# Merging two 256-column products into one of 512 columns in 18 dense halves of a decoder trunk

## The reference

```
x_n = rms_norm(x);  h = x_n @ w_in                     # 1024 x 9216
y_a = (a_gb * conv3(a_gc * a_val)) @ w_out_a
u   = conv31(glu_val * sigmoid(glu_gate)) + conv_b_b
y_b = silu(layer_norm(u)) @ w_out_b + b_out_b
y_x = cross_attention(q, rms_norm(mem), w_kv) @ w_out_x
merged = g0 * y_a + g1 * y_b + g2 * y_x                # g = sigmoid(h_gate + b_gate)
x = x + merged @ w_o
x = x + hierarchical_moe(rms_norm(x));  out = rms_norm(x)
```

## Time and profile before

| | us |
|---|---|
| median of three runs | 865.9 |
| profiled execution | 865.89 |
| its span, first to last instruction | 864.1 |
| PE busy | 850.9 (98%) |
| DVE busy | 786.9 (91%) |
| ACT busy | 648.4 (75%) |
| POOL busy | 25.4 (3%) |

### The profile page before, as it was taken

How to read it: one execution, slowest core, us unless ns; L and a number is a source line. 1 busy time by engine, 2 the same in 40 slices (tenths; PEclk the granted TensorE clock), 3 DMA queues, 4 the chain that set the end, 5 groups by cost and what they waited for, 6 DMA issues and landing times.

```text
span 864.1 us, 14576 instructions
## 1 busy us (share of the span) xinstructions
PE 850.9 (98%) x5734; PEld 753.0 (87%) x5734; DVE 786.9 (91%) x779; ACT 648.4 (75%) x631; POOL 25.4 (3%) x33
## 2 busy tenths in 40 slices
PE   9999999999999999999999999999999999999996
PEld 6999999999889999877788888888888888888874
DVE  6458999999987786789999999999999999999996
ACT  6563424344454366588999999999999999999996
POOL 0110000000000000017000000000000000000000
PEclk9999999999999999999999999999999999999999
DMA  9962555445452359647999999999999999999971
GB/s 355 428 222 98 194 194 195 174 159 179 173 195 98 133 177 420 234 182 267 393 421 431 424 430 429 426 429 430 428 427 431 429 426 432 429 425 430 429 308 49
DMA packets 20743, 270.68 MB, mean 313 GB/s; under 512 B 2272, under 2 KB 2528, under 8 KB 4448
## 3 DMA queue, kind: packets, MB, share of 16 engines
q1 hardware_dynamic: 20144, 268.31, 76.1%
q10 hardware_dynamic: 560, 1.84, 0.5%
HBM read 269.08 MB, written 1.05 MB: 313 GB/s over the span
## 4 chain that ended last, share of the span: by engine, by line
PE 84%; DVE 12%; issue 2%; DMA 1%; ACT 0%; SPq 0%; DVEq 0%; ACTq 0%
PE ps L1614 24%; PE ps L1628 12%; PE ps L1428 9%; PE ps L1430 9%; PE ps L1429 9%; PE ps L1599 4%; PE ps L1638 3%; DVE lo L1132 3%; DVE lo L857 2%; DVE conv L956 2%; PE ps L1444 2%; PE ps L1445 2%; PE ps L1443 2%; PE ps L1712 2%; PE ps L1719 1%
## 5 line engine op out<-in xcount | busy, mean ns | idle before, releaser
L1132 DVE TENSOR_TENSOR lo<-raw,hi 128x2048 fp32r<-128x2048 f32 x142 | 320.1, 2295 | 0.3 <-ACT hi L670 0.3
L670 ACT ACTIVATE hi<-raw 128x2048 fp32r<-128x2048 f32 x141 | 264.8, 1914 | 15.7 <-PE ps L1614 15.7
L459 ACT ACTIVATE hi<-raw 128x2048 fp32r<-128x2048 f32 x62 | 118.6, 1914 | 58.4 <-PE ps L1430 37.6
L857 DVE TENSOR_TENSOR lo<-raw,hi 128x2048 fp32r<-128x2048 f32 x61 | 139.3, 2287 | 20.2 <-ACT hi L459 18.9
L1428 PE MATMUL ps<-inA,hi 128*128 128x256 f32 x544 | 155.0, 285 | 1.4 <-DVE lo L857 1.4
L1614 PE MATMUL ps<-hi,xeT 128*128 128x512 f32 x384 | 154.4, 402 | 0.2
L1429 PE MATMUL ps<-inA,hi 128*128 128x256 f32 x544 | 153.9, 283 | 0.0
L1430 PE MATMUL ps<-inA,lo 128*128 128x256 f32 x544 | 153.9, 283 | 0.0
L1614 PE MATMUL ps<-lo,xeT 128*128 128x512 f32 x384 | 150.2, 391 | 0.0
L1132 DVE TENSOR_TENSOR lo_last<-raw,hi_last 128x2048 fp32r<-128x2048 f32 x48 | 110.3, 2298 | 0.0
L1428 PEld LDWEIGHTS ps<-inA,hi 128*128 128x128 f32 x544 | 104.4, 192 | 2.5 <-DVE lo L857 2.4
(11 more groups left out here) (259 smaller groups left out, 1291.8 us busy)
## 6 DMA issues: line engine op xcount, KB each, us to landing
raw<-in_w_experts SPq DMA_DIRECT2D x96, 2048.0 KB, 12.2
raw<-in_w_dense SPq DMA_DIRECT2D x28, 2048.0 KB, 7.8
raw<-in_w_dense SPq DMA_DIRECT2D x3, 1024.0 KB, 12.1
x_sb<-in_x SPq DMA_DIRECT2D x2, 512.0 KB, 3.6
raw<-in_w_dense SPq DMA_DIRECT2D x2, 512.0 KB, 7.7
mem_sb<-in_mem SPq DMA_DIRECT2D x1, 1024.0 KB, 15.7
x_again<-in_x ACTq DMA_DIRECT2D x1, 1024.0 KB, 17.4
out<-x SPq DMA_DIRECT2D x3, 256.0 KB, 2.1
```

The costliest lines, as they stand in the source:

```text
L459: return nc.scalar.activation(conv_half(hi, N), raw_half(slot, h), ACT.Copy)
L670: nc.scalar.activation(expert_half(hi, N0), raw_flat(slot, k % 2), ACT.Copy).then_inc(hi_made, 1)
L857: nc.vector.tensor_tensor(conv_half(lo, N), raw_half(slot, h), conv_half(hi, N).bitcast(f32), ALU.subtract).then_inc(lo_made, 1)
L1132: nc.vector.tensor_tensor(expert_half(lo, N0), raw_flat(expert_slot(m), k % 2), expert_half(hi, N0).bitcast(f32), ALU.subtract).then_inc(l ...
```

## The change

- `inA` and `inB` become [k, part, position], so that a k tile's high and low part are 512 neighbouring columns.
- In the halves named in `WIDE` (2 to 7 and 44 to 55) `wide_columns` takes the place of `columns`: the weight's high part is multiplied with both activation parts at once, 512 columns that fill a whole PSUM bank, and the weight's low part with the activation's high part, 256 columns, into the bank's first half. A half then has 32 products instead of 48, and its result lies in two banks, in two column halves that have to be added.
- The six banks are used as three pairs by the wide halves (`bank_pair`).
- The sum: ScalarE copies the second column half out (for glu_value and out_b with the bias) and counts `low_part`; VectorE adds the first column half and frees the banks. For glu_gate and gate1 ScalarE then applies the sigmoid to the sum, behind `dense_hi(n + 3)`. VectorE's product with the gate reads SBUF.
- In a wide step VectorE makes `lo` of half n + 2 before it takes the half's result, not behind it, and `ln_variance` goes ahead of both.

```diff
+WIDE = [n for n in range(2, DENSE) if UNITS[n // 2][0] in ("glu_value", "glu_gate", "out_x", "gate1", "out_b")]
-        inA = at("inA", A0, [2, KT, T], r32)
+        inA = at("inA", A0, [KT, 2, T], r32)
...
+            def wide_columns(N, acts):
+                w_hi, w_lo = conv_half(hi, N), conv_half(lo, N)
+                for c in range(2):
+                    bank = ps[:, 2 * bank_pair(N) + c, :]
+                    for k in range(KT):
+                        mm(bank, w_hi[:, k, c * P:(c + 1) * P], acts[:, k, :, :].rearrange("p x t -> p (x t)"),
+                           start=(k == 0), stop=False, skip_group_check=True)
+                        last = mm(bank[:, 0:T], w_lo[:, k, c * P:(c + 1) * P], acts[:, k, 0, :],
+                                  start=False, stop=(k == KT - 1), skip_group_check=True)
+                last.then_inc(half_used, 1)
... (ScalarE)
+                elif name == "gate1":
+                    act.wait_ge(merged_x, 4)
+                    nc.scalar.activation(gate[:, two, :], wide_half(n, 1), ACT.Copy).then_inc(low_part, 1)
...
                 elif name == "out_b":
+                    act.wait_ge(half_used, n + 1)
...
+                    for k in range(2):
+                        last = nc.scalar.activation(part[:, k, :], wide_half(n, 1)[:, k, :], ACT.Identity,
+                                                    bias=vec("b_out", 2 * q4 + k))
+                    last.then_inc(low_part, 1)
                     act.wait_ge(merged_all, q4 + 1)
...
                 if n + 3 <= DENSE + 1 and n != F["gate1"] + 1:
                     dense_hi(n + 3)
+                if name in ("glu_gate", "gate1"):
...
+                    act.wait_ge(gate_summed, gate_sums(n) + 1)
+                    for k in range(2):
+                        last = nc.scalar.activation(gate[:, 2 * q4 + k, :], gate[:, 2 * q4 + k, :], ACT.Sigmoid,
+                                                    bias=vec(vector_, 2 * q4 + k, k0))
... (VectorE)
+                if n in WIDE:
+                    dense_lo(n + 2)
+                    b = 2 * bank_pair(n)
...
+                    dve.wait_ge(low_part, WIDE.index(n) + 1)
+                    nc.vector.tensor_tensor(dst, wide_half(n, 0), dst, ALU.add).then_inc(bank_free[b], 1)
...
-                if not (name == "w_o" and n % 2 == 1):
+                if n not in WIDE and not (name == "w_o" and n % 2 == 1):
                     dense_lo(n + 2)
```

More of the change, by code:

```diff
@@ L255, in sums, with bank_pair, banks_of, bank_uses @@
             return ps[:, 2 * t:2 * t + 2, :].rearrange("p a b -> p (a b)")
+        def bank_pair(n):
+            return (n - 1) % BANK_PAIRS
+        def banks_of(n):
+            return (2 * bank_pair(n), 2 * bank_pair(n) + 1) if n in WIDE else (n % RING,)
+        def bank_uses(n, b):
+            return sum(b in banks_of(m) for m in range(n))
+        def wide_half(n, part_):
+            b = 2 * bank_pair(n)
+            return ps[:, b:b + 2, part_ * T:(part_ + 1) * T]
         def raw_slot(u):
@@ L440, in _, with gate_sums @@
             ins.then_inc(rounds_made, 1)
+        def gate_sums(n):
+            return sum(UNITS[m // 2][0] in ("glu_gate", "gate1") for m in WIDE if m < n)
         def stage_of(n):
@@ L660, in _ @@
                     dense_hi(n + 3)
+                if name in ("glu_gate", "gate1"):
+                    vector_, k0, made = ("b_glu", 1, glu_gate) if name == "glu_gate" else ("b_gate", 1, gate_made)
+                    act.wait_ge(gate_summed, gate_sums(n) + 1)
+                    for k in range(2):
+                        last = nc.scalar.activation(gate[:, 2 * q4 + k, :], gate[:, 2 * q4 + k, :], ACT.Sigmoid,
+                                                    bias=vec(vector_, 2 * q4 + k, k0))
+                    last.then_inc(made, 1)
                 for work in extra.get(n, ()):
@@ L1046, in _ @@
                 two = slice(2 * q4, 2 * q4 + 2)
-                if name in ("a_c", "a_b", "out_a", "out_x", "out_b"):
+                if name in ("a_c", "a_b", "out_a"):
                     dve.wait_ge(half_used, n + 1)
+                if n in urgent:
+                    urgent[n]()
+                if n in WIDE:
+                    dense_lo(n + 2)
+                    b = 2 * bank_pair(n)
+                    dst = part[:, :, :] if name in ("out_x", "out_b") else (u_sb if name == "glu_value" else gate)[:, two, :]
+                    dve.wait_ge(low_part, WIDE.index(n) + 1)
+                    nc.vector.tensor_tensor(dst, wide_half(n, 0), dst, ALU.add).then_inc(bank_free[b], 1)
+                    dve.wait_ge(bank_free[b], bank_uses(n, b) + 1)
+                    dve.sem_inc(bank_free[b + 1], 1)
+                    if name == "glu_value":
+                        dve.sem_inc(glu_value, 1)
+                    elif name in ("glu_gate", "gate1"):
+                        dve.sem_inc(gate_summed, 1)
                 if name == "a_c":
@@ L1080, in _ @@
                     dve.wait_ge(gate_made, 8 + q4 + 1)
-                    for k in range(2):
-                        c = 2 * q4 + k
-                        link(nc.vector.scalar_tensor_tensor(part[:, k, :], bank2[:, k, :], vec("b_out", c),
-                                                            gate[:, c, :], ALU.add, ALU.mult))
-                    dve.sem_inc(bank_free[b], 1)
+                    link(nc.vector.tensor_tensor(part[:, :, :], part[:, :, :], gate[:, two, :], ALU.mult))
                     nc.vector.tensor_tensor(merged[:, two, :], merged[:, two, :], part[:, :, :], ALU.add).then_inc(merged_all, 1)
```

128 lines of the change are left out of this document (73 added, 55 removed).

## The result

The changed kernel takes **876.94 us**, median of 5 runs (874.97 to 878.61), against 865.9 before: a ratio of 1.0129, 95% interval 1.0119 to 1.0140. It is slower, as forecast, but by 11.0 us instead of 6.5, and the time lies outside the range of 868.5 to 875.5. The runs differ by 3.6 us among themselves, where those of the kernel before differ by 1.5, and their order is that of the mean granted clock: 878.61 and 878.40 us at 0.988, 876.94 at 0.992, 875.21 and 874.97 at 0.995.

What follows compares the result with a forecast made beforehand. TensorE was taken to bound the dense part. Against 865.89 us: -3.8 products, -0.4 old wait, +5.7 first wait, +3.5 second wait, +1.4 clock, +0.1 restarts, in all +6.5, so 872.4 us; range 868.5 to 875.5.

Steps and rivals of the forecast that it cites:

- The clock: Gap before half 52: granted clock falls late in it, a quarter of half 52's 5.5 us at half rate, +1.4 us.
- the clock stays up: Rival: no fall of the clock in the gap before half 52, all else as forecast, 871.0 us; chance 0.30.
- The products: 18 halves (2 to 7, 44 to 55): each 5.55 us instead of 5.76, 0.21 less, in all -3.8 us.
- The old wait: Before half 49: TensorE's wait for VectorE's remainder goes, as that is now made ahead of the sum, -0.4 us.
- the restart: Before half 49: 0.1 us for TensorE to start again after its wait there.
- The first wait: Before half 52: TensorE waits for `lo`, late behind gate1's sigmoids and half 49's sum, +5.7 us.
- The second wait: Before half 57: out_b's merges turn every 6.96 us against TensorE's 5.55, so TensorE waits, +3.5 us.
- The front halves: Halves 2 to 7: they lose nothing of the 1.25 us that their wider products save.
- One to one: End of the dense part: its delay moves the experts' start by as much; their stage keeps its length within a microsecond.

Runs made afterwards that it cites:

- the products grouped: Changed kernel, but each column block runs its eight 512-column products first, then its eight 256-column ones, instead of alternating: 875.77 us, one run.
- the changed order at half 49: Changed kernel, but VectorE makes branch b's low part and half 52's `lo` ahead of half 49's sum instead of behind it: 875.28 us.
- the short series of products of ones: Changed kernel plus small products of ones, 24 ahead of half 52 and 10 ahead of half 57, ending inside the waits: 873.14 us.
- long ones: Changed kernel plus small products of ones, 40 ahead of half 52 and 20 ahead of half 57, overrunning both waits: 876.05 us.
- 14 products of ones ahead of half 52: Added to the changed kernel with `lo` ahead of half 49's sum and out_b's `lo` behind the merge: 875.39 us, against 870.38 without them.

## Why the prediction was wrong

The account of the profiled execution is +12.7 us where the forecast had +6.5. That is the slowest of the five; the median is +11.0, and against it the clock counts 3.8 us and not 5.8.

**The clock (forecast 1.4, measured 5.8).** This is the step that failed. The prediction took "a quarter" of one half at half rate and one fall, and put the second wait's fall at nothing without saying why; there were two, and each lasted on through most of the half behind its wait: half 52 took 8.46 us where it takes 5.64 to 5.72 at the full clock, 2.8 more, and half 57 8.41 instead of 5.44, 3.0 more. Both lie at the dear end of what the traces show. With the clock falling in the same waits, half 52 took 7.36 us with the products grouped, 7.48 with out_b as before and 6.99 with the changed order at half 49, which is 1.3 us more than at the full clock, so the size taken for one fall could happen and the missing second fall was the surer mistake. Two more mistakes lie in it. That "the fall would come late in the gap" was read off one fall, 3.7 us after the last product, and here it came after 2.2 us, in a gap of 6.4. And the cost was tied to the gap, when it lies behind it: a low clock costs nothing while TensorE waits, and it didn't come back until 6.1 us after the first product of half 52 and of half 57. The upper end that the prediction itself gave for one fall, 5.5 us, was not reached either. In the median, against the kernel with the short series of products of ones, the clock is worth 3.8 us. The rival "the clock stays up" (chance 0.30) fell with it: it gave 871.0, and with the clock held up the time is 873.1. The Trainium skill (page "TensorE: Matmul & The Clock Gate", section "Part 1: The HAM clock gate"), cited there for the drop to half rate in idleness, agrees with both falls.

**The products (forecast -3.8, measured -2.2).** The 0.21 us a half came true at the faster of the two rates (halves 46 and 47, 5.55 us each); at the slower one, in the first six and in out_b, a half saved 0.11. The price was bounded correctly (0 to 7.7), and its value, put together from two pitches measured in streams of one width, is that of the faster rate. Twelve of the 18 halves ran at the slower one, 0.107 us dearer each, which is 1.3 of the 1.6 us missing. The Trainium skill's 2.5 ns (the same page, section "Back-to-back issue gap"), by which all would have gained 0.7 us, doesn't fit these products: by it halves 2 to 7 would have gained 0.24 (96 mergers, an estimate too), and they gained 0.64.

**The old wait (forecast -0.4, measured -0.66).** It went as described; with it went the restart.

**The first wait (forecast 5.7, measured 7.1).** Cause, place and length are right: half 49's sum at 328.97 (forecast 328.6), half 52's `lo` done at 334.40 (333.7), TensorE done at 328.1 (328.0). The experiment with the changed order took 2.6 us off it. Of the 1.4 that were missing, some 0.85 are small delays along the chain, among them VectorE waiting for its own sum (0.25 before L1051). The other 0.52 are a wait that I had not looked for: half 51's `lo` begins at 319.96 instead of 319.44 and TensorE waits 0.36 us for it at 322.29. I followed the chain of branch b and not the `lo` between.

**The second wait (forecast 3.5, measured 3.2).** Right, with the turn of 6.96 us as worked out from rows. The merges at 345.60 and 366.50 are 3 x 6.97 apart. Placing `lo` behind the merge ended it.

**The front halves** "lose nothing of their 1.25 us". They gained half of that, 0.64, and in the changed kernel passed it on. Half 2 began another 0.46 us sooner, but among the traces of these kernels its start lies anywhere from 22.50 to 24.05, so I give that no cause. By themselves they are worth nothing that can be measured, as half 49 hangs on a chain of VectorE's that did not move.

**One to one.** The experts' first product and the last instruction came 12.73 and 12.71 us later. The claim held.

Had the prediction used 5.8 for the clock and 2.2 for the products, its other terms would have given 865.9 - 2.2 - 0.4 + 5.7 + 3.5 + 5.8 + 0.1 = 878.4, against 878.6 in the profiled execution; some of that is luck, as the start of half 2 (-0.46) and the missed wait (+0.5) cancel. Against the median, 3.8 for the clock alone makes 872.4 + 2.4 = 874.8, and with 2.2 for the products 876.4 of the 876.9 measured.

## What to carry to other kernels

When a change opens a wait on a busy TensorE, price the wait and, as a term of its own, the work behind it at the lower clock, once for every wait; here that was 2.8 and 3.0 us after gaps of 6.4 and 3.1 us in the changed kernel's trace, and from 1.3 us up in the others. A split that saves TensorE a few per cent by giving two other engines an exchange for every half is decided by the order of their queues: write down one turn of the exchange and compare it with TensorE's turn (6.96 against 5.65 here; 5.6 with one instruction moved). And take a pitch from the pattern that will run, in more than one place: the same alternation ran here at 5.55 and at 5.65 us a half.

## What the runs showed of the hardware

- The fall of the granted clock came 2.2 and 2.3 us after the last product here and 3.7 in the kernel before, and 4.4 us after it with the changed order at half 49, when TensorE had been multiplying again for 0.6 us; the low stretches in the dense part lasted 3.4 to 10.2 us in the traces. The same kernel ran with mean clocks of 0.988 to 0.995, and its time moved by 3.6 us with them; with products of ones in the waits it moved by 0.9 (short series) or 0.35 us (long ones).
- A product of ones with 128 columns in this type is executed as two of 0.11 us, as long as one of 256 columns of the dense part (0.12).
- Products of 512 columns took 0.230 us in groups of eight, and this case's experts have 0.227. Alternating with products of 256 columns, a pair took either 0.353 or 0.347 us, and kept the one or the other until something stood between.
- Filling a wait can cost more than it gives: with 14 products of ones ahead of half 52, half 52 gained 2.4 us, and a stop of 1.3 us two halves on and a microsecond more ahead of the experts took it back.
